# A 64-byte constant tile declared after the activation tiles instead of before them: every tensor between the two places starts 64 bytes lower

## The reference, cut to what matters

```
h = rms_norm(x, attn_norm_w);  x = x + hybrid_mixer(h, ...)
h = rms_norm(x, moe_norm_w);   x = x + hier_moe(h, ...)      # 32 experts, 2 of 8 in one of 4 groups
x = x + sigmoid(rms_norm(x, ple_norm_w) @ w_ple_gate) * (p @ w_ple);  x = rms_norm(x, final_norm_w)
for i in range(4):
    x = x + mixer_i(rmsnorm(x, norm_mix_g[i]))               # conv, neighbourhood attention, hyena, conv
    g, u = split(rmsnorm(x, norm_ffn_g[i]) @ w13[i], 2)
    x = x + (silu(g) * u) @ w2[i]                            # "ffn0" to "ffn3"
```

## The kernel before

| tensor | first byte before | remainder by 256 |
|---|---|---|
| ring_hi / ring_lo | 41088 / 65664 | 128 |
| x_res | 90240 | 128 |
| neg_half (64 bytes) | 98432 | 128 |
| h_hi / h_lo | 98496 / 106688 | 192 |
| ident_sb, params | 114880, 115904 | 192 |
| inv | 118528 | 0 |
| eps_col | 118560 | 32 |
| work area | 118592 | 64 |

## Time and profile before

### The profile page before, as it was taken

How to read it: one execution, slowest core, us unless ns; L and a number is a source line. 1 busy time by engine, 2 the same in 40 slices (tenths; PEclk the granted TensorE clock), 3 DMA queues, 4 the chain that set the end, 5 groups by cost and what they waited for, 6 DMA issues and landing times.

```text
span 2041.0 us, 32534 instructions
## 1 busy us (share of the span) xinstructions
PE 1933.4 (95%) x13424; PEld 1757.9 (86%) x13424; DVE 1375.7 (67%) x1569; ACT 923.1 (45%) x990; POOL 46.3 (2%) x65
## 2 busy tenths in 40 slices
PE   6999997998999979999999999998988999999999
PEld 6998887776777769999989999996878999999998
DVE  4768975766677665766667655567997555666555
ACT  4544744654556553443344443334343333434342
POOL 0000000000000000001101000000000000000000
PEclk9999998999999999999999999999999999999999
DMA  7552342866677746555554375553324555555553
GB/s 225 178 168 89 110 152 103 294 263 246 248 291 288 283 158 182 163 177 194 185 179 131 104 224 186 190 177 106 104 66 159 174 191 191 169 165 166 188 200 106
DMA packets 243915, 366.03 MB, mean 179 GB/s; under 512 B 12566, under 2 KB 217961, under 8 KB 231401
## 3 DMA queue, kind: packets, MB, share of 16 engines
q1 hardware_dynamic: 243817, 364.64, 53.3%
HBM read 363.57 MB, written 1.05 MB: 179 GB/s over the span
## 4 chain that ended last, share of the span: by engine, by line
PE 58%; DVE 13%; DMA 6%; ACT 5%; issue 3%; DVEq 0%; POOL 0%; ACTq 0%
PE proj L931 30%; PE acc L1265 11%; PE proj L950 6%; DMA raw<-in_w_exp_up_dram 6%; PE proj L1448 3%; DVE ring_lo L2425 3%; DVE ring_lo L3108 2%; PE acc L1418 2%; ACT ring_hi L2152 1%; ACT second_hi L2152 1%; ACT ring_hi L1864 1%; DVE second_lo L3108 1%; PE acc L1524 1%; PE acc L1278 1%; PE proj L1716 1%
## 5 line engine op out<-in xcount | busy, mean ns | idle before, releaser
L2425 DVE TENSOR_TENSOR ring_lo<-raw,ring_hi 128x2048 fp32r<-128x2048 f32 x242 | 560.1, 2317 | 227.9 <-ACT ring_hi L1864 227.4
L1864 ACT ACTIVATE ring_hi<-raw 128x2048 fp32r<-128x2048 f32 x242 | 462.1, 1913 | 465.6 <-PE proj L931 215.8
L931 PE MATMUL proj<-h_hi,ring_hi 128*128 128x256 f32 x1808 | 518.9, 287 | 12.3 <-DVE ring_lo L2425 7.2
L931 PE MATMUL proj<-h_hi,ring_lo 128*128 128x256 f32 x1808 | 506.7, 280 | 0.0
L931 PE MATMUL proj<-h_lo,ring_hi 128*128 128x256 f32 x1808 | 506.4, 280 | 0.0
L931 PEld LDWEIGHTS proj<-h_hi,ring_hi 128*128 128x128 f32 x1808 | 340.8, 188 | 25.2 <-issue 13.9
L931 PEld LDWEIGHTS proj<-h_lo,ring_hi 128*128 128x128 f32 x1808 | 341.2, 189 | 4.2 <-issue 3.2
L931 PEld LDWEIGHTS proj<-h_hi,ring_lo 128*128 128x128 f32 x1808 | 340.9, 189 | 0.0
L931 PE MATMUL proj<-g_hi,ring_hi 128*128 128x256 f32 x704 | 195.4, 278 | 4.5 <-DVE hid L2958 4.5
L931 PE MATMUL proj<-g_lo,ring_hi 128*128 128x256 f32 x704 | 194.6, 276 | 0.0
L931 PE MATMUL proj<-g_hi,ring_lo 128*128 128x256 f32 x704 | 194.5, 276 | 0.0
(11 more groups left out here) (440 smaller groups left out, 3434.0 us busy)
## 6 DMA issues: line engine op xcount, KB each, us to landing
raw<-in_f_w_dram SPq DMA_DIRECT2D x132, 1024.0 KB, 5.0
raw<-in_w_exp_gate_dram SPq DMA_DIRECT2D x32, 1024.0 KB, 4.8
raw<-in_w_exp_up_dram SPq DMA_DIRECT2D x32, 1024.0 KB, 5.1
raw<-in_w_exp_down_dram SPq DMA_DIRECT2D x32, 1024.0 KB, 4.8
raw<-in_w_in_dram SPq DMA_DIRECT2D x29, 1024.0 KB, 5.1
raw<-in_a_w_in_dram SPq DMA_DIRECT2D x24, 1024.0 KB, 5.2
raw<-in_b_w_qkv_dram SPq DMA_DIRECT2D x12, 1024.0 KB, 5.2
raw<-in_c_w_in_dram SPq DMA_DIRECT2D x12, 1024.0 KB, 5.1
```

Source lines behind the costliest of these rows:

```text
L931: last = pe.matmul(bank[:, a, :], w[:, k, a * P:(a + 1) * P], h[:, k, :], start=(k == 0 and w is hi and h is h_h and (a == 0 or not first) ...
L1864: act.activation(w_hi[n.slot][:, :], raw[n.slot][:, :], ACT.Copy).then_inc(hi_ready, 1)
L2425: dve.tensor_tensor(w_lo[n.slot][:, :], raw[n.slot][:, :], w_hi[n.slot][:, :].bitcast(f32), SUB)\
```

## The change

`neg_half` is declared after `inv` instead of before `h_hi`. Of it:

```
-        neg_half = sb("neg_half", [P, 16])
         h_hi = sb("h_hi", [P, KT, SEQ], f32r)
...
         inv = sb("inv", [P, TT])
+        neg_half = sb("neg_half", [P, 16])
         eps_col = sb("eps_col", [P, 1])
```

## The result

| | before | after |
|---|---|---|
| median | 2035.91 us (2033.43 to 2042.81) | 2055.73 us (2051.49 to 2060.33, 5 runs) |
| profiled execution, its span | 2042.81, 2041.0 us | 2061.14, 2059.3 us |
| mean granted clock in it | 0.987 | 0.982 |

The ratio after / before is 1.0089, 95% interval 1.0061 to 1.0116, which is 12.4 to 23.6 us. The forecast was no change, 2035 us; the time measured lies inside its range of 2014 to 2058, near the slower rival's centre of 2055.

A forecast was written before the change was run, and what follows sets the result against it. TensorE, busy 95% of the span, was taken to bound the kernel. The terms were all 0 except -1 us for the experts' products, taking the median from 2035.9 to 2035 us, with an 8-in-10 range of 2014 to 2058.

The forecast's parts named there:

- slower rival: Product_f with h, loops above all: equal remainders collide, third level 4.6 ns slower; 2046 to 2063 us, centre 2055; chance 0.29.
- What bounds the kernel: Whole kernel: TensorE is busy 95% of the span, so one matmul's cost decides; two pitches, 4.6 ns apart.
- Step 1: Product_f with h (L931), 5424 matmuls: no change of pitch, 0 us, with ends of 25 us gained or lost.
- Step 2: Product_t with h, 960 matmuls, at both pitches before: taken as 0, with ends of 2.2 us either way.
- Step 3: The experts' 384 products with h: -1 us, between 2.5 us gained and 1.8 us lost.
- Steps 4 to 6: 176 turns with ident, GpSimd's reads of neg_half, VectorE and ScalarE reads of h, params and ident: 0 each.
- Faster: Product_f with h loses its long pitch, ffn1 and ffn2 pass 369: 2011 to 2026 us, centre 2018; chance 0.29.
- The ports are independent, timing alone: TensorE's pitch comes from timing, not addresses; h stays or flips here and there: 2036 us, give or take 5; chance 0.12.
- The signs named: Matmuls per 50 us: 359 in ffn1/ffn2, 369 in ffn0/ffn3; experts' median falling towards 391 ns; L931 mean near 287 ns.

The follow-up runs named there:

- experiment 8: Not the full kernel: TensorE's products alone, streams at nine distances from the weights, 256 and 512 columns, everything else left out; one execution, 372.25 us.
- Experiment 1: Against the kernel before, h alone moved to remainder 128, with ident, ones and params left in place; 2054.61 us, ratio 1.0074.
- experiment 4: Against the kernel before, ring_hi, ring_lo and x_res moved 64 bytes up to h's remainder 192, h left in place; 2064.28 us, ratio 1.0131.
- experiment 3: Against the kernel before, small tiles placed ahead of h put it at remainder 64, where g is; 2026.24 us, ratio 0.9947.
- experiment 10: The kernel with h at remainder 64 timed again on another chip with more runs, against the kernel before; 2027.23 us, ratio 0.9951.
- experiment 5: Against the kernel before, h_hi at remainder 128, equal to the ring's, while h_lo stays at 192; 2049.42 us, ratio 1.0048.
- experiment 7: Against the kernel before, ring_lo alone moved to remainder 192, with ring_hi at 128 and h at 192; 2057.37 us, ratio 1.0085.
- experiment 9: Products alone again: distances repeated plus 256 bytes, then two streams or two weight tiles in turn; one execution, 283.75 us.

## Why the prediction was wrong, step by step

**What bounds the kernel: right.** TensorE's pitch is what the kernel costs: 15.0 of the 18.3 us between the two profiled executions are steps from start to start of matmuls without an interruption. The two levels were read rightly. One reading names the wrong rows: that both levels occur for the same addresses is shown by `attn` and `product_t`, not by the ffn parts, where each tile kept to one level.

**Step 1, product_f with h, taken as 0: this is the step that failed.** It was bounded by 25 us either way and then valued by the nearest row, the experts' 512-column products, where d = 0 is "at any rate not dear". That row was of another form, and the form decides: alone, the step from d = 64 to 0 costs 512 columns nothing (228.7 ns at both), as the row said, while it takes 256 columns from 113.3 or 117.8 to 120.0 ns. At 192 the ranking is turned round: 233.4 ns, dear, for 512 columns, and 113.7 or 117.8, cheap, for 256 (experiment 8). The text even held the warning, that this form ranks d = -64 last where L931 has it short, and used the row all the same. In its place the runs show a third level at d = 0, held throughout L931 with h: +2.17 ns x 5424 = +11.8 us, where the prediction had 0.

**Step 2, product_t with h, taken as 0, with ends at 2.2 us: wrong, and outside its ends.** L950 too is a 256-column product, and it had d = -64, the good distance, before. A third level was thought of for product_f and not for this, where even the slower rival stops at the long pitch. Measured: 4.40 ns x 960 = +4.2 us.

**Step 3, the experts, -1 us: right in sign.** The median durations fell from 397.5 to 390 ns, and the pitch by 4.65 ns: 384 x 4.65 = 1.8 us.

**Steps 4 to 6, turns, GpSimd, VectorE and ScalarE, nothing: right.** Experiment 1 leaves ident, ones and params where they were and has the whole loss. L3108 reads 2292 and 2290 ns for the rows; the page has VectorE at 1376.0 us against 1375.7, ScalarE at 922.7 against 923.1, GpSimd at 46.3 in both. The lines of the earlier trace rows with neg_half have a median of 2900 ns (`rate`) and 693 ns (`inv`).

**The rivals.** *Slower* had the mechanism: a third level at equal remainders, on L931 with h, the loops above all. Its place is shown (experiments 1 and 4), its time was near (2055 against 2055.73), but by luck, through two errors that cancel: the step is 2.2 ns and not 4.6, so the count is 353 and not 349, and the time that this leaves out came from L950 (4.2 us, where the rival had 2) and from what separates two runs. *Faster* fell: the long pitch of h is indeed due to its place relative to the ring, but d = 0 is worse, and the cure is d = -64, shown in experiments 3 and 10. *The ports are independent, timing alone* falls with experiment 8. The Trainium skill, "TensorE: Matmul & The Clock Gate", section "What happens when you issue a matmul", says that the two read ports are independent and that loading the next weights doesn't take bandwidth from the running matmul; here the trace doesn't agree with what the prediction drew from it, that the operands' addresses can't matter: with nothing else at work the pitch goes from 113.3 to 120.0 ns with their distance. By the page the time would have been 2036 us, 20 under what was measured.

**The signs named** did their work: 370 in ffn0 and ffn3 kept timing out of it, 353 and 354 in ffn1 and ffn2, 5 or 6 under the 359 forecast, showed the direction, and the experts' median fell. The mean duration of L931 went to 290 ns from 287, where it was to stay.

**What stays open.** Which structure has this period isn't known from these runs; they show a period of 256 bytes, effects down to 16 bytes, and the dear distances 0, 96 and 128. Which product of a mixed row of three pays isn't settled (experiments 5, 7 and 9 don't fit one rule). What decides between 113.3 and 117.8 ns at d = 64 and -64 is open too. In experiment 8 the same loop on the same tiles differs between the passes only in what ran before it, so that is the likely cause; no run was made for it. Nor is a level always kept until an interruption: at 192 the first pass began with five steps of 118 to 123 ns and then held 113.3.

## What to carry to other kernels

Where TensorE is busy nearly all the time and loads weights for each matmul, count matmuls in equal busy stretches at full clock, tile by tile: if two tiles in the same loop differ, their placing relative to the weights is worth a try, since it costs no instruction (here 64 bytes, from remainder 64 to 128, decided between 2027 and 2056 us). Choose the distance by measuring the very form, in columns and type, that runs most often; a wider form ranked the distances otherwise, and was the row that misled this forecast. When small tiles are added or moved in a list of declarations, keep the large operands' addresses fixed, or an edit can bring a change of time (1.3% at most in these runs) that has nothing to do with what it was made for.

## What the runs showed of the hardware

- With weights loaded for every matmul (fp32r, 128 x 128, 256 columns) the pitch is 113.3, 117.8 or 120.0 ns and some values between, by the distance of stream and stationary operand modulo 256 bytes: 272 to 288 cycles for 256 columns, with no other engine at work (experiments 8 and 9).
- The same addresses can run at either of two pitches (d = 64: 113.3 and 117.8 ns), each held over a run of 96 matmuls; d = 192 and 16 had two as well. d = 0 and 96 had one pitch each time.
- For 512 columns the range is 228.7 to 234.2 ns, the best distances are 0 and 64, and -64, with 64 the best for 256 columns, is among the dear ones.
- The median durations in whole ns follow the pitch (276 to 277 ns at 113 to 114 ns, 279 to 281 at 117.8, 283 at 120.0); the two decimals of a timeline, 0.28 us, hide it. Starts and counts give it directly.
